# Sample attention of a hybrid decoder step: a fourth buffer for gathered cache rows, gathers issued behind the window loads, and the Silu of the output gate after the stage

## The chip, the core and the metric

The kernel runs on one NeuronCore of a Trainium2 chip. Five engines work side by side, each with its own instruction queue: TensorE (PE) multiplies and transposes into PSUM, VectorE (DVE) and ScalarE (ACT) do elementwise work, GpSimd (POOL) does elementwise work and issues the gathers, and SyncE (SP) issues the plain transfers. They meet at semaphores. The metric is the time of one launch in microseconds.

## What is computed

One step of a decoder trunk: a prompt of 512 tokens and eight samples of one new token each go through an input projection, sparse attention in three branches, a Mamba-2 scan (SSD), an output projection and an MLP. The change lies in the attention of the eight samples. Each sample reads its selected rows out of a paged cache, and its window rows out of a buffer:

```python
full_s = jnp.concatenate([paged_rows(cache_s), kv_s], axis=1)
idx = select_blocks(p_cmp, qpos, -(-(past + T) // SEL_BLOCK))
o_sel = selected_attention(q, idx, full_s, qpos)
win_rows = jnp.concatenate([win_buf.astype(x.dtype), kv_w], axis=1)
o_win = window_attention_rows(q, win_rows, qpos, kpos)
attn = gate_branches(gates, o_cmp, o_sel, o_win)
...
y = y.reshape(B, L, D_INNER) * jax.nn.silu(z.astype(f32))   # SSD output gate
```

PAST_LEN is 1024, WINDOW is 512, there are 16 heads over 4 key/value groups of 64 columns, all in float32. Of the past of a sample every block but one is selected, so a gather fetches all 1024 rows of the sample and a mask drops one block.

## The kernel before, in words

The program is written by hand, engine by engine: each engine's instructions run in the order in which its functions are written, and every crossing between engines is a semaphore wait. There is no scheduler.

The prompt's attention (`att_pe`, `att_act`, `att_dve`) ends at about 896 us of the span. The samples' stage (`smp_pe`, `smp_act`, `smp_dve`, `smp_sp`, `smp_pool`) follows it, and then the scan (`ssd_pe` and its kin), the output projection and the MLP.

For sample b the stage needs two tiles. The **gathered rows** (2 MB, 16 KB in each of 128 partitions) come by an indirect DMA that POOL issues (L1425). They have three places: `SEL = (sel_t[:, 0], sel_x, sel_t[:, 1])`, place b % 3. The **window rows** (1 MB) come by four plain DMAs that SP issues (L1408 and L1411) into `win_t`, which has three places too. Both kinds of transfer for sample b wait until `values(b - 3)` has been done on PE (`n_v`), since it is the last reader of the place.

PE runs a loop over the samples. In pass b it does: `fill(b + 1)`, that is six groups of four 128x128 transposes which turn the keys of the next sample (groups 0 to 3 from the gathered rows, 4 and 5 from the window rows, L1466); `turn_p(b)`, which transposes the probabilities (L1485); `scores(b + 1)` (L1476); `values(b)` (L1495). The six groups of `fill` use three PSUM banks in turn. Each is copied out before group x + 3 may start: the even groups by ACT (`key_copy`, L1574), the odd ones by DVE (L1628). ACT also takes the exponentials (L1579), copies the output of the sample before (`out_copy`, L1611) and the turned probabilities (L1597); DVE adds the mask and takes the maximum (L1681, L1686).

Work of the scan is laid into the passes. PE transposes pieces of the convolved input: `xs_turn` (L2163), eight `x_chunk_turn` (L2170), two `b_turn` (L2180) and `c_turn` (L2186). DVE scales the eight chunks (`x_scaled`, L2024), which also frees PSUM bank 7 for the next piece; ACT copies the two `b_turn` results (`b_copy`, L2114) and applies Silu to the eight tiles of the gate z, two in each of the passes 3 to 6 (L1587). After the loop DVE works out the factors of the three branches (`part_factors`, L1732 to L1765), PE computes `c_products` (L2193) and the samples' outputs (L1549, L1555), and the scan starts with `chunk(0)` (L2216). POOL prepares selector tiles for the scan (`ssd_pool`, L1877 to L1885) in memory that the gathered rows have left.

## Time and profile before

| | us |
|---|---|
| median of 3 runs | 2793.37 |
| lowest, highest | 2791.44, 2794.19 |
| the profiled execution, as timed | 2792.03 |
| its span in the profile | 2790.3 |
| PE busy | 2645.6 (95%) |
| DVE, ACT, POOL busy | 1128.8, 854.6, 107.3 |

The page of the profile cuts the span into 40 slices of 70 us. PE is busy for nine tenths or more in nearly all of them; the slices at 840 to 1120 us are those with 7 and 8 tenths, and the samples' stage from 896 to 1003 us is in these. The times below are positions in the span, read from the timelines of the engines. A row of a timeline gives start, duration, engine, line, operation, tiles and count; square brackets at its end hold how long the engine sat idle before it, and what ended that.

### The profile page before, as it was taken

How to read it: one execution, taken by the hardware profiler on the slowest of the kernel's cores; microseconds unless marked ns; L12 is line 12 of the kernel's file. 1: busy time of each engine (PE TensorE's matmuls, PEld its weight loads, DVE VectorE, ACT ScalarE, POOL GpSimd, SP SyncE). 2: the span in 40 equal slices, each digit the busy share in tenths (PEclk: the TensorE clock that was granted, in tenths of full speed). 3: DMA queues.
4: the chain of work that ended last, by engine and by line, in shares of the span. 5: the costliest groups of instructions: out<-in, count | busy, mean ns of one | idle time of the engine just before them, and what ended most of it. 6: DMA issues, size and time to landing. Idle time of an engine off the chain costs nothing.

```text
span 2790.3 us, 50995 instructions
## 1 busy us (share of the span) xinstructions
PE 2645.6 (95%) x21237; PEld 2531.0 (91%) x21237; DVE 1128.8 (40%) x1703; ACT 854.6 (31%) x1373; POOL 107.3 (4%) x116
## 2 busy tenths in 40 slices
PE   7889999998699788999999999999999999999998
PEld 6779999998577557998999999999999999999998
DVE  4432224554676577433333333333333233333333
ACT  3242112223575445322212212222122122221233
POOL 0000000000000041110000000000000000000011
PEclk9999999999799888999999999999999999999999
DMA  5154333233003743322322222222222222222222
GB/s 214 61 171 152 96 90 90 74 100 101 3 31 95 221 140 123 97 91 77 95 90 93 90 90 90 90 90 90 94 94 90 90 90 90 90 90 93 94 90 86
DMA packets 241815, 274.64 MB, mean 98 GB/s; under 512 B 19397, under 2 KB 233811, under 8 KB 237494
## 3 DMA queue, kind: packets, MB, share of 16 engines
q1 hardware_dynamic: 238966, 237.88, 27.3%
q0 software_dynamic: 1728, 33.56, 3.2%
q10 hardware_dynamic: 1040, 2.10, 0.3%
q8 instruction: 54, 0.88, 0.1%
q14 instruction: 27, 0.22, 0.0%
HBM read 261.10 MB, written 20.71 MB: 101 GB/s over the span
## 4 chain that ended last, share of the span: by engine, by line
PE 60%; DVE 2%; ACT 1%; issue 1%; DMA 0%; POOL 0%; ACTq 0%; POOLq 0%; DVEq 0%
PE PS L677 58%; DMA sel_x<-in_cache_kv_sel,idx_s 0%; PE PS L2735 0%; ACT sqr L2648 0%; ACT w_hi L658 0%; PE PS L2337 0%; DVE dec L2072 0%; DVE tmp_s L2307 0%; PE PS L2483 0%; DVE ys L2310 0%; ACT u_hi L2650 0%; DVE u_lo L2666 0%; DVE relu L2661 0%; PE PS L2216 0%; PE PS L2256 0%
## 5 line engine op out<-in xcount | busy, mean ns | idle before, releaser
L664 DVE TENSOR_TENSOR w_lo<-w_raw,w_hi 128x1024 fp32r<-128x1024 f32 (+1 forms) x388 | 460.3, 1190 | 1321.8 <-ACT w_hi L658 1320.8
L658 ACT ACTIVATE w_hi<-w_raw 128x1024 fp32r<-128x1024 f32 (+1 forms) x388 | 395.5, 1024 | 1481.1 <-PE PS L677 1480.8
L677 PE MATMUL PS<-h_hi,w_hi 128*128 128x260 f32 x3360 | 675.5, 283 | 8.0 <-DVE h_lo L591 3.6
L677 PE MATMUL PS<-h_lo,w_hi 128*128 128x260 f32 x3360 | 674.9, 282 | 0.0
L677 PE MATMUL PS<-h_hi,w_lo 128*128 128x260 f32 x3360 | 673.8, 282 | 0.0
L677 PEld LDWEIGHTS PS<-h_hi,w_hi 128*128 128x128 f32 x3360 | 516.3, 189 | 9.3 <-DVE h_lo L591 3.7
L677 PEld LDWEIGHTS PS<-h_lo,w_hi 128*128 128x128 f32 x3360 | 519.0, 189 | 0.0
L677 PEld LDWEIGHTS PS<-h_hi,w_lo 128*128 128x128 f32 x3360 | 517.8, 189 | 0.0
L677 PE MATMUL PS<-u_hi,w_hi 128*128 128x260 f32 x2048 | 411.1, 282 | 8.4 <-DVE u_lo L2666 8.4
L677 PE MATMUL PS<-u_lo,w_hi 128*128 128x260 f32 x2048 | 410.5, 282 | 0.0
L677 PE MATMUL PS<-u_hi,w_lo 128*128 128x260 f32 x2048 | 410.0, 281 | 0.0
L677 PEld LDWEIGHTS PS<-u_hi,w_hi 128*128 128x128 f32 x2048 | 313.7, 188 | 10.0 <-issue 10.0
L677 PEld LDWEIGHTS PS<-u_lo,w_hi 128*128 128x128 f32 x2048 | 315.3, 188 | 0.0
L677 PEld LDWEIGHTS PS<-u_hi,w_lo 128*128 128x128 f32 x2048 | 314.8, 188 | 0.0
L677 PE MATMUL PS<-mix_hi,w_hi 128*128 128x260 f32 x512 | 103.4, 284 | 7.5 <-DVE w_lo L664 7.5
L677 PE MATMUL PS<-mix_lo,w_hi 128*128 128x260 f32 x512 | 103.3, 283 | 0.0
L677 PE MATMUL PS<-mix_hi,w_lo 128*128 128x260 f32 x512 | 103.0, 283 | 0.0
L2556 DVE TENSOR_TENSOR x_acc<-PS,x_acc 128x520 f32 (+1 forms) x144 | 93.5, 691 | 11.2 <-PE PS L677 11.2
L677 PEld LDWEIGHTS PS<-mix_hi,w_hi 128*128 128x128 f32 x512 | 79.1, 190 | 7.6 <-issue 7.6
L1280 ACT ACTIVATE prob<-PS,negmax 128x128 f32<-128x128 f32 (+3 forms) x128 | 65.8, 525 | 49.3 <-DVE negmax L1310 49.3
L677 PEld LDWEIGHTS PS<-mix_lo,w_hi 128*128 128x128 f32 x512 | 79.5, 190 | 0.0
L677 PEld LDWEIGHTS PS<-mix_hi,w_lo 128*128 128x128 f32 x512 | 79.3, 190 | 0.0
(449 smaller groups left out, 2326.9 us busy)
## 6 DMA issues: line engine op xcount, KB each, us to landing
w_raw<-in_w_up SPq DMA_DIRECT2D x256, 256.0 KB, 2.8
w_raw<-in_w_down SPq DMA_DIRECT2D x256, 256.0 KB, 2.9
w_raw<-in_w_in SPq DMA_DIRECT2D x160, 256.0 KB, 2.9
w_raw<-in_w_out SPq DMA_DIRECT2D x64, 256.0 KB, 3.0
out_kv_win_s<-in_state_kv_win SPq DMA_DIRECT2D x8, 1022.0 KB, 7.5
win_t<-in_state_kv_win SPq DMA_DIRECT2D x8, 896.0 KB
xtok<-in_x_prompt SPq DMA_DIRECT2D x4, 1024.0 KB, 8.2
st_s<-in_state_ssm SPq DMA_DIRECT2D x8, 512.0 KB, 4.9
```

What stands on the lines that cost most here:

```text
L658: ins = e.activation(hi, raw, ACT.Copy)
L664: ins = e.tensor_tensor(lo, raw, hi.bitcast(F32), ALU.subtract)
L677: mm = e.matmul(PS[:, bank + 2 * m + h, 0:HN], w, x[:, k0 + k, h * HN:h * HN + HN], start=st and c == 0, stop=sp and c == 2)
L1280: e.activation(prob[:, u % 2, P_OFF[qt]:P_OFF[qt] + w], PS[:, qt, 0:w], ACT.Exp, bias=negmax[:, u % 2, qt:qt + 1], accum_out=den[:, u % 2, ...
L2556: e.tensor_tensor(x_acc[:, tile], PS[:, bank:bank + 2, 0:HN], x_acc[:, tile], ALU.add).then_inc(g_out, 1)
```

## The change

1. **A fourth place.** `sel_y` lies in memory that later holds `xdt`, the output of `x_scaled`. The places are now `SLOT = (0, 1, 2, 3, 0, 1, 2, 0)` for samples 0 to 7. The gather for sample 3 goes into `sel_y` and waits for the end of the prompt's attention (`as_o`), no longer for `values(0)`.
2. **Order of the gathers.** The gathers for samples 4, 5 and 6 wait for `values` 0, 1 and 2 (the samples that held places 0, 1 and 2), the one for sample 7 for `values(4)`. Each of these four also waits until the window load of the sample before it (3, 4, 5, 6) has landed. The waits of the window loads themselves are as they were.
3. **Silu after the stage.** The eight Silu instructions leave passes 3 to 6 and run on ACT after the last `out_copy`.
4. **The scan's pieces are laid out anew.** Since `xdt` may be written only after `values(3)`, the two `b_turn` come first (after `values(2)` and in pass 3), and the chunk turns run in passes 4 to 7, the last two of them in pass 7. DVE's `x_scaled` moves with them: chunks 6 and 7 are scaled inside `part_factors`. `ssd_pool` waits for `values(6)` in place of `values(5)`.

```diff
-        SEL = (sel_t[:, 0], sel_x[:], sel_t[:, 1])
+        sel_y = at("sel_y", [P, 8, KVW], A0 + 8 * TILE)
+        SEL = (sel_t[:, 0], sel_x[:], sel_t[:, 1], sel_y[:])
+        SLOT, USE = (0, 1, 2, 3, 0, 1, 2, 0), (1, 1, 1, 1, 2, 2, 2, 3)
...
             for b, dead in enumerate((2 * NU, 4 * NU - 8, 4 * NU)):
                 e.wait_ge(*as_s(dead))
-                gather(b, b)
-            for b in range(3, NB):
-                e.wait_ge(n_v, b - 2)
-                gather(b, b % 3)
+                gather(b, SLOT[b])
+            e.wait_ge(as_o, NH // 2)
+            gather(3, SLOT[3])
+            for b in range(4, NB):
+                e.wait_ge(n_v, SLOT.index(SLOT[b], 4 if b == 7 else 0) + 1)
+
+                e.wait_ge(nw_ld[(b - 1) % NS], 64 * ((b - 1) // NS + 1))
+                gather(b, SLOT[b])
...
-                elif 3 <= b < 7:
-                    x_chunk_turn(e, 2 * b - 5)
-                elif b == 7:
+                elif b == 3:
                     b_turn(e, 1)
-                    c_turn(e)
-                    e.transpose(PS[0:NB, 0, 0:96], stat[QR, 0, :], ident[QR, QR])
-                    e.transpose(PS[0:NB, 0, 96:192], stat[QR, 1, :], ident[QR, QR]).then_inc(n_stT.sem, 1)
+                elif b >= 4:
+                    if b == 7:
+                        e.transpose(PS[0:NB, 0, 0:96], stat[QR, 0, :], ident[QR, QR])
+                        e.transpose(PS[0:NB, 0, 96:192], stat[QR, 1, :], ident[QR, QR]).then_inc(n_stT.sem, 1)
+                    x_chunk_turn(e, 2 * b - 8)
+                    if b == 7:
+                        x_chunk_turn(e, 7)
+                        c_turn(e)
...
-                elif 2 <= b < 6:
-                    x_chunk_turn(e, 2 * b - 4)
-                elif b == 6:
+                elif b == 2:
                     b_turn(e, 0)
+                elif 4 <= b < 7:
+                    x_chunk_turn(e, 2 * b - 7)
...
-                elif 3 <= b < 7:
-                    for k in (2 * b - 6, 2 * b - 5):
-                        e.activation(pt[:, T_Z + k, :], pt[:, T_Z + k, :], ACT.Silu).then_inc(f_z.sem, 1)
-                elif b == 7:
+                elif b == 3:
                     b_copy(e, 0)
...
             out_copy(e, NB - 1)
+            for k in range(8):
+                e.activation(pt[:, T_Z + k, :], pt[:, T_Z + k, :], ACT.Silu).then_inc(f_z.sem, 1)
...
-                elif 3 <= b < 7:
-                    x_scaled(e, 2 * b - 6)
+                elif b >= 5:
+                    x_scaled(e, 2 * b - 9)
...
-                elif 3 <= b < 7:
-                    x_scaled(e, 2 * b - 5)
+                elif 4 <= b < 7:
+                    x_scaled(e, 2 * b - 8)
...
             ch.step(e.tensor_tensor(two(fac_T[:, 64:96]), two(den_s[:]), both(gate_b[:, :, 2]), ALU.mult))
+            x_scaled(e, 6)
+            x_scaled(e, 7)
             e.wait_ge(n_e, 1)
...
-            e.wait_ge(n_v, 6)
-            for x, count in enumerate((3, 3, 2)):
+            e.wait_ge(n_v, 7)
+            for x, count in enumerate((3, 2, 2, 1)):
```

POOL's queue, the gathers for samples 2 to 7, before (`n_v` counts `values`; the number behind a tile's name is its allocation):

```order
L1425 DMA sel_t_166<-in_cache_kv_sel,idx_s_55 128x4096 [waits pe_done_1]
L1425 DMA sel_t_166<-in_cache_kv_sel,idx_s_55 128x4096 [waits n_v]
L1425 DMA sel_x_167<-in_cache_kv_sel,idx_s_55 128x4096 [waits n_v]
L1425 DMA sel_t_166<-in_cache_kv_sel,idx_s_55 128x4096 [waits n_v] x2
L1425 DMA sel_x_167<-in_cache_kv_sel,idx_s_55 128x4096 [waits n_v]
```

The same place of POOL's queue now (`nw_ld0` to `nw_ld2` count the window loads landed in each of their three places):

```order
L1427 DMA sel_t_166<-in_cache_kv_sel,idx_s_55 128x4096 [waits pe_done_1]
L1427 DMA sel_y_168<-in_cache_kv_sel,idx_s_55 128x4096 [waits as_o]
L1427 DMA sel_t_166<-in_cache_kv_sel,idx_s_55 128x4096 [waits nw_ld0,n_v]
L1427 DMA sel_x_167<-in_cache_kv_sel,idx_s_55 128x4096 [waits nw_ld1,n_v]
L1427 DMA sel_t_166<-in_cache_kv_sel,idx_s_55 128x4096 [waits nw_ld2,n_v]
L1427 DMA sel_t_166<-in_cache_kv_sel,idx_s_55 128x4096 [waits nw_ld0,n_v]
```

The gather for sample 3 has moved from behind `values(0)` to the end of the prompt's attention, and the four behind it have a second wait each.

ACT's queue, pass 4 of the samples' loop, before (`pr` is the exponential, `o_t` the output copy, `proj` the gate z under Silu, `kT` the key copies, `prT` the turned probabilities):

```order
L1579 ACT_TABLE_LOAD
L1579 ACTIVATE pr_180,stat_177<-pr_180,stat_177 96x512 [waits n_max]
L1611 ACTIVATE o_t_168<-PS 96x256 [waits n_v]
L1587 ACT_TABLE_LOAD
L1587 ACTIVATE proj_64<-proj_64 128x520 x2
L1574 ACTIVATE kT_179<-PS 128x512 [waits n_fill,pe_done_1]
L1574 ACTIVATE kT_179<-PS 128x512 [waits n_fill] x2
L1597 ACTIVATE prT_181<-PS 128x384 [waits n_v,n_pT]
```

The same pass now:

```order
L1589 ACTIVATE pr_181,stat_178<-pr_181,stat_178 96x512 [waits n_max]
L1621 ACTIVATE o_t_169<-PS 96x256 [waits n_v]
L1584 ACTIVATE kT_180<-PS 128x512 [waits n_fill,pe_done_1]
L1584 ACTIVATE kT_180<-PS 128x512 [waits n_fill] x2
L1604 ACTIVATE prT_182<-PS 128x384 [waits n_v,n_pT]
```

Two table loads and two Silus have left the pass, and the key copies stand right behind the output copy.

DVE's queue from the last maximum to the wait for ACT's exponentials in `part_factors`, before (`st8` to `f_T_s` are the factors, `xdt` the scaled chunks):

```order
L2024 TENSOR_TENSOR xdt_208<-PS,dta_218 128x4x128 [waits d_pe_done]
L1681 TENSOR_TENSOR pr_180<-PS,dropq_174 96x512 [waits n_pT,pe_done_1]
L1686 TENSOR_REDUCE stat_177<-pr_180 96x1 [waits n_add]
L1732 COPY st8_191<-PS 8x192 [waits n_pe_end]
...
L1742 RECIPROCAL den_s_185<-st8_191 8x32
L1744 TENSOR_TENSOR f_T_s_189<-den_s_185,gate_b_178 8x32 [waits dve_ch]
L1746 TENSOR_TENSOR es_s_190<-e_s_187,st8_191 8x64 [waits n_e]
```

The same place now:

```order
L1691 TENSOR_TENSOR pr_181<-PS,dropq_175 96x512 [waits n_pT,pe_done_1]
L1696 TENSOR_REDUCE stat_178<-pr_181 96x1 [waits n_add]
L2036 TENSOR_TENSOR xdt_209<-PS,dta_219 128x4x128 [waits d_pe_done]
L1742 COPY st8_192<-PS 8x192 [waits n_pe_end]
...
L1752 RECIPROCAL den_s_186<-st8_192 8x32
L1754 TENSOR_TENSOR f_T_s_190<-den_s_186,gate_b_179 8x32 [waits dve_ch]
L2036 TENSOR_TENSOR xdt_209<-PS,dta_219 128x4x128 [waits d_pe_done] x2
L1758 TENSOR_TENSOR es_s_191<-e_s_188,st8_192 8x64 [waits n_e]
```

Three scalings now stand behind the last maximum, two of them between the factors.

## Rows read from the trace of the kernel before

**Rows 1.** Chain that ended last, in order of time: start us, us, what

```profile
968.42 13.68 DMA sel_x<-in_cache_kv_sel,idx_s
...
1097.04 152.96 PE PS L677 x1269
```

**Rows 2.** Timeline of PE through the samples' stage

```profile
943.96 0.66 PE L2170 MATMUL PS<-ident,proj 128*128 128x128 f32 x4
948.39 3.67 PE L1466 MATMUL PS<-ident,sel_x 128*128 128x128 f32 x16 [3.77 <-DMA sel_x<-in_cache_kv_sel,idx_s]
...
962.13 0.66 PE L1466 MATMUL PS<-ident,sel_t 128*128 128x128 f32 x4 [1.97 <-ACT kT L1574]
...
968.07 0.66 PE L2170 MATMUL PS<-ident,proj 128*128 128x128 f32 x4
970.88 3.58 PE L1466 MATMUL PS<-ident,sel_t 128*128 128x128 f32 x16 [2.15 <-DMA sel_t<-in_cache_kv_sel,idx_s]
...
979.79 0.66 PE L2170 MATMUL PS<-ident,proj 128*128 128x128 f32 x4
982.14 2.22 PE L1466 MATMUL PS<-ident,sel_x 128*128 128x128 f32 x16 [1.70 <-DMA sel_x<-in_cache_kv_sel,idx_s]
...
989.64 0.66 PE L2180 MATMUL PS<-ident,proj 128*128 128x128 f32 x4
```

**Rows 3.** Timeline of POOL, the gather of sample 3, the scan's first and fourth instruction

```profile
919.49 0.94 POOL L1425 DMA_INDIRECT sel_t<-in_cache_kv_sel,idx_s  x1 [33.01 <-PE PS L1495]
...
982.66 1.81 POOL L1877 MEMSET sel_h<- 128x2048 f32 x1 [13.31 <-issue]
...
989.57 1.17 POOL L1885 TENSOR_SCALAR_AFFINE_SELECT sel_p<-sel_p 16x1024 f32<-16x1024 f32 x1
```

**Rows 4.** Timeline of SP's queue, window loads of samples 0 and 5

```profile
896.18 1.11 SPq L1408 DMA_DIRECT2D win_t<-in_state_kv_win  x3
...
944.07 1.90 SPq L1408 DMA_DIRECT2D win_t<-in_state_kv_win  x3
```

**Rows 5.** Gathers of samples 2, 5 and 6: count, us from issue to landing

```profile
sel_t<-in_cache_kv_sel,idx_s POOLq DMA_INDIRECT x1, 8.6
...
sel_t<-in_cache_kv_sel,idx_s POOLq DMA_INDIRECT x1, 14.0
...
sel_t<-in_cache_kv_sel,idx_s POOLq DMA_INDIRECT x1, 12.3
```

**Rows 6.** DMA queues in 921:923, 944:946, 946:948: packets, MB, share of 16 engines

```profile
q1 hardware_dynamic: 81, 0.66, 103.9%
...
q0 software_dynamic: 41, 0.43, 52.3%
...
q0 software_dynamic: 2, 0.02, 2.8%
```

**Rows 7.** Timeline of ACT, pass 4 and the end of the stage

```profile
959.14 1.28 ACT L1587 ACT_TABLE_LOAD   x1
960.43 1.16 ACT L1587 ACTIVATE proj<-proj 128x520 f32<-128x520 f32 x2
...
1005.71 0.87 ACT L2128 ACTIVATE ebc<-PS 128x384 f32<-128x384 f32 x2 [9.58 <-PE PS L2202]
```

**Rows 8.** Timeline of DVE, a scaled chunk and the end of the factors

```profile
986.05 0.69 DVE L2024 TENSOR_TENSOR xdt<-PS,dta 128x512 f32<-128x512 f32 x1
...
995.13 0.28 DVE L1760 TENSOR_TENSOR pnz<-den_s,ident 8x128 f32<-8x128 f32 x1
```

**Rows 9.** PE's first reading of window rows, and its statistics transposes

```profile
904.42 1.95 PE L1466 MATMUL PS<-ident,win_t 128*128 128x128 f32 x8
...
991.60 0.25 PE L1534 MATMUL PS<-ident,stat 96*8 96x96 f32 x1
```

**Rows 10.** Windows: us, busy (x) by engine, PEclk, DMA share, GB/s

```profile
965.00:980.00 15.00, 12.79 (x110) 8.79 (x105) 6.36 (x10) 8.30 (x13) 0.94 (x1) 0.89 0.98 318
...
972.00:974.00 2.00, 2.00 (x11) 2.00 (x10) 0.69 (x1) 0.95 (x2) 0.00 (x0) 0.50 1.15 299
```

More of the change, by code:

```diff
@@ L1386, in build_program @@
         smn = at("smn", [P, 2], MF + 11360)
-        n_ld = [sem(f"n_ld{x}") for x in range(3)]
+        n_ld = [sem(f"n_ld{x}") for x in range(4)]
         nw_ld = [sem(f"nw_ld{x}") for x in range(NS)]
@@ L1992, in xs_scaled @@
             x = xdt_s[half]
-            e.wait_ge(*d_xT(half + 1))
+            e.wait_ge(*d_xsT(half + 1))
             ch.settle()
@@ L2022, in x_scaled @@
             c, half = f // 2, f % 2
-            e.wait_ge(*d_xT(f + 3))
-            e.tensor_tensor(xdt_c(c)[:, 4 * half:4 * half + 4], by_pair(PS[:, 7, :]),
+            e.wait_ge(*d_xT(f + 1))
+            e.tensor_tensor(xdt_c(c)[:, 4 * half:4 * half + 4], by_pair(PS[:, 4 if f == 7 else 7, :]),
                             per_head(dta[:, c, 0, 8 * half:8 * half + 8]).to_broadcast([P, 4, 2, HD]),
@@ L2163, in xs_turn @@
                 last = e.transpose(PS[0:NB, 7, x * P:x * P + P], xa[:, 4 * half + x, SEQ:NT], ident[:])
-            last.then_inc(d_xT.sem, 1)
+            last.then_inc(d_xsT.sem, 1)
         def x_chunk_turn(e, f):
             c, half = f // 2, f % 2
-            e.wait_ge(*d_xdt(f + 2))
+            if f == 0:
+                e.wait_ge(*d_btok(2))
+            elif f < 7:
+                e.wait_ge(*d_xdt(f + 2))
+            else:
+                e.wait_ge(n_ev_a, 3 * NB)
+                e.wait_ge(n_ev_d, 3 * NB)
             for x in range(4):
-                last = e.transpose(PS[:, 7, x * P:x * P + P], xa[:, 4 * half + x, c * P:c * P + P], ident[:])
+                last = e.transpose(PS[:, 4 if f == 7 else 7, x * P:x * P + P],
+                                   xa[:, 4 * half + x, c * P:c * P + P], ident[:])
             last.then_inc(d_xT.sem, 1)
@@ L2174, in b_turn @@
             e.wait_ge(*d_xa(12))
[L2175 removed]
             if f:
[L2177 to L2178 removed]
+                e.wait_ge(*d_btok(1))
+            else:
+                e.wait_ge(*d_xdt(2))
             for x in range(4):
[L2180 removed]
+                last = e.transpose(PS[:, 7, x * P:x * P + P],
                                    xa[:, 8 + x % 2, (2 * f + x // 2) * P:(2 * f + x // 2) * P + P], ident[:])
```

42 lines of the change are left out of this document (20 added, 22 removed).

## The prediction

> **What bounds the kernel now.** I read the chain of waits first, since it says which work sets the end. From 1097 us on it is all PE, and right before the scan it runs through one transfer: the gather for sample 7, issued at 968.42 and landed 13.68 us later [rows 1]. So the end of the samples' stage moves the end of the kernel one for one: behind it stand chains of PE, DVE and ACT with no slot in time of their own. The question is only when that stage ends.
>
> Next the timeline of PE through the stage. Write F(b) for the start of `fill(b)` and V(b) for the end of `values(b)`, which is where the next transposes start. The rows give V(2) = 943.96, F(4) = 948.39, V(4) = 968.07, F(6) = 970.88, V(5) = 979.79, F(7) = 982.14 and V(6) = 989.64 [rows 2]. Three fills begin late because a gather is late: 3.77 us at F(4), 2.15 at F(6), 1.70 at F(7), 7.6 us in all. A fourth wait is ACT's: in `fill(5)` the fourth group stands 1.97 us for a key copy [rows 2], and ACT was then busy with a table load of 1.28 us and two Silus of 1.16 us [rows 7].
>
> A pass costs, when nothing is late: F(7) to V(6) is 7.50 us, and a chunk turn of 0.66 behind it makes 8.2. After a long stop it costs more: F(6) to V(5) is 8.91 us [rows 2], and the granted clock there is 0.50, that is 1.2 GHz, though it is 1.00 elsewhere in the pass [rows 10].
>
> Last the transfers. A gather is 128x4096 floats (2.1 MB), a window load half of that, so a sample needs 3.15 MB. The stretch 965 to 980 shows the 16 engines 0.98 busy at 318 GB/s [rows 10]: 3.15 MB take 9.9 us, more than the 8.2 us of a free pass. Alone a gather lands after 8.6 us; beside a window load it takes 12.3 to 14.0 us [rows 5]. In 921 to 923, right after sample 3's gather was issued along with a window load, all the traffic is the window's (q1, 0.66 MB) [rows 6]. **So once the waits are gone the transfers are the next bound.** That decides the size of the gain.
>
> **The change part by part.**
>
> *Gather 3 early.* It now leaves at about 896.2, with the window loads of samples 0 to 2 [rows 4]. With its own 2.1 MB and three window loads the engines have 5.3 MB to move, 17 us at 318 GB/s, so it is down by 914, before V(0), and is read only two passes later. Gain by itself: nothing, since gather 3 was in time. What it buys is the idle time of the transfers that followed, for gathers 4 to 6.
>
> *Gathers 4 to 6.* Gather 4 needs V(0), about 919.2 (sample 3's gather left at 919.49 on it [rows 3]), and window load 3, issued then. No row shows a window load alone to its landing; bounds are 4 us (1.05 MB at 318 GB/s with the start left out) and 9 (the longest gather less the rate above). I take 6.5, since its data would be through in four to five. Gather 4 leaves at about 926 and lands by 936, where it is wanted at V(2) + 0.66 = 944.6. So F(4) moves from 948.39 to 944.6. `b_copy(0)` stands before the key copies in that pass, 0.55 us, and the turn of 1.16 us for two Silus is not there. V(3) = 944.6 + 7.5 + 0.55 = 952.7, say 953. Gather 5 leaves when window load 4 has landed, at about 941, and shares the engines with window load 5 from 945 on [rows 4]. By its own 8.6 us it lands at 949.6, by 12.3 at 953.3. F(5) = 953.0 to 953.5. No Silu stands before its key copies, so the 1.97 us go, and **V(4) = 953.3 + 7.5 = 961, against 968.07**.
>
> *Gather 6, the place where it is decided.* It leaves when window load 5 is down, at about 954, along with window load 6 (issued at V(3)). A pair takes 12.3 to 14 us: it lands at 966.3 to 968. F(6) would want it at 961.7. The window load of sample 7 goes out at V(4) = 961, into this gather's last third. What does an arriving window load do to a gather under way? The nearest row: in 944 to 946, with window load 5 just begun, the gather of sample 4 moved 0.43 MB, and in the 2 us after that only its last 0.02 MB [rows 6]. These last packets came late, but they were few. If the gather keeps its place, 966.3; if it stands still for the whole window load (1.05 MB, 3.3 to 4.2 us), 970.5. I take **F(6) = 967.5**, nearer the first, since the rows show two packets delayed and no large part of a gather. PE has then stood 5.9 us, and I charge the pass at its slow length of 8.91 us: V(5) = 976.4, and with the chunk turn F(7) can be 977.1.
>
> *Gather 7.* It waits for V(4) as before; window load 6 is down by then or 2 us later. It leaves at 961.2 to 963, five to seven us before 968.42 [rows 1]. But gather 6 and window load 7 are ahead of it: from 967 less the landing, 966, another 9.9 us and some 0.8 to land give 976.7. So **F(7) = 977.1 against 982.14: 5.0 us gained**, PE and transfers arriving together. V(6) = 984.6.
>
> *The end of the stage.* DVE has three scalings of 0.69 us [rows 8] behind the last maximum where it had none: the fifth waits for the chunk turn behind `values(6)`, the others stand between the factors. Two of them lie before the last factor, 1.38 us, which was done at 995.4 [rows 8]. Against this the statistics transposes stand ahead of the other turns and no longer at 991.60 [rows 9]: 0.75 us earlier. Net +0.65 us on the way to the factors. PE itself has one 0.6 us turn more before `values(7)`. Either way **0.7 us lost**; bounds 0 (both covered) and 1.4 (nothing of the order helps).
>
> *Silu.* Eight of them are 4 x 1.16 = 4.6 us, with a table load of 1.28 before and one after: 7.2 us of ACT. They stand in the 9.58 us in which ACT waited for the scan's first product [rows 7]. Covered with 2.4 us to spare, and the results are wanted 70 us later. If that cover went, up to 7.2 us would be on the path. The Trainium skill, page "ScalarE: Activation LUTs", section on what a table load costs, puts a switch at about 2.66 us, since a drain goes with the load of 1.28. The trace shows the load, and Silu starting 0.01 us after it. By the page the eight Silus and two switches are 9.9 us, and the scan would start some 0.4 us later; the sum would be that much worse.
>
> *POOL.* `ssd_pool` now waits for V(6) and not V(5). Its four instructions ran from 982.66 to 990.74 [rows 3], 8.1 us; from V(6) = 984.6 they end at 993, and the scan's first product, seen by ACT at 1005.71 [rows 7], comes at about 1001. Covered by 8 us. Behind the gathers with their new waits POOL has nothing else queued.
>
> **Sum:** 5.0 - 0.7 = 4.3 us. The profiled execution took 2792.03 (span 2790.3), which would become 2787.7 (2786.0). The median is 2793.37, 1.3 above it; 2793.37 - 4.3 = **2789.1 us**. About 0.2%, 5.6 us, is what a measurement can tell from no change, so this is inside it.
>
> **The rivals.**
>
> *A. The transfers pair up well.* Gather 6 lands at 965.5, the clock stays up (pass 8.2), and gather 7 takes from V(4) what it takes now: 961 + 0.2 + 13.68 = 974.9. Then F(7) = 975, gain 7.2 - 0.7 = 6.5: 2786.9, and 2786 at best. For it: 13.68 us already includes a window load beside it and a rest of gather 6. Against it: gather 6 would have to be through by 965, and 9.9 us for each pair leave no room.
>
> *B. Engines share packet by packet.* The Trainium skill, "DMA: Bandwidth & Descriptors", section on queues, rings and completion order, says that each DMA engine goes round the queues that have work, a packet at a time. The trace does not agree in the first 2 us of a pair, where the gather gets nothing [rows 6], but may for one under way. As a mechanism here: gather packets are 16 KB (0.43 MB with small ones among 41) against 8 KB of the window loads (0.66 MB in 81), so a gather would take two thirds. Gather 6 keeps moving and lands at 967. But window load 0, read at 904.42 [rows 9], now has gather 3 beside it from 898: at a third of the rate its remaining 0.9 MB take 9 us and not 3; it lands at 907 to 908, and everything behind it shifts by up to 3.6 us. The passes shift; gather 7, wanted at about 980, comes with them. Gain 5.0 - 0.7 - 2.5 to 3.6 = 0.7 to 1.8: 2792.
>
> *C. Slower: window loads starve gather 6.* If each window load takes the engines for its whole life of 9 us (small pieces included), gather 6 stands from 962 to 970 and lands at 973. F(6) is 973.2 against 970.88 now, V(5) 982.1, F(7) 982.8, the end 0.6 + 0.7 = 1.3 us later: 2794.7; with B's shift added, 2797. It decides from F(6) = 971.6 on: 971.6 + 8.91 + 0.66 - 982.14 + 0.7 = -0.3, about even. For it: the first 2 us of a pair. Against it: the gather of sample 6 moved on while the next window load began, and landed after 12.3 us.
>
> *D. Nothing moves.* If landing of the window loads is slow (9 us or more), gathers 4 and 5 leave at 928 and 943, gather 5 is 2 us late and gather 6 leaves at 957: F(6) = 970, F(7) = 980. Gain 2 - 0.7 = 1.3: 2792.
>
> **How the numbers follow.** The forecast (F(6) between 966 and 969, gain 3 to 5.6) 0.48; A 0.22; B and D together 0.22; C 0.08. The forecast's own range is 2787.8 to 2790.4. Eight in ten takes in A to its best end and D, B, and C's near part: 2786.0 to 2794.6. Faster by over 5.6 us is most of A: 0.23. Slower by over 5.6 us needs C and B together: 0.04. The rest, 0.73, is within 0.2%.
>
> **What would show it.** In the profile after: the first DMA stall of PE at F(6), of 3 to 8 us, and none at F(4); V(4) at 960 to 962; at F(7) a stall under 2 us; key copies in `fill(5)` without the 2 us wait; ACT's idle time before the scan's first exponential down from 9.58 to 1 to 3 us; the last factor of DVE 6.4 us after V(6). The transfers should be busy without a gap from 955 to 976. I am wrong in size if F(6) is before 965 or after 971, and in mechanism if PE's first window transposes (904.42) come later, if the scan waits for ACT or POOL, or if gather 5 is late by more than 1 us.

## The result and the profile after

The changed kernel takes 2796.99 us (median of 20 runs, 2790.87 to 2799.87) against 2793.34 for the kernel before, run beside it on the same chip (20 runs, 2787.70 to 2797.26). The ratio is 1.0012, with an interval of 1.0006 to 1.0017: some 3.5 us slower, less than the 0.2% within which the forecast counts a time as the same, but on the other side of zero, and outside both of the forecast's ranges (2787.8 to 2790.4, and the wide one, 2786.0 to 2794.6). The profiled execution took 2799.59 us, with a span of 2797.9, which is 2.6 us above its own median; the one of before was 1.3 below its median. So the two traces are 7.6 us apart where the medians are 3.7 apart, and I use the traces to place the loss, and the medians for its size.

The first view is again the chain of waits (start us, us, what). It still goes through the gather of sample 7. In the kernel before it then stays on PE until the scan; now it runs through DVE behind the stage, and for longest through two steps on `den_s`:

```profile
967.80 12.03 DMA sel_t<-in_cache_kv_sel,idx_s
...
994.75 2.01 DVE den_s L1760
996.78 1.20 DVE den_s L1762
...
1104.21 184.99 PE PS L677 x1536
```

`den_s` is a tile of 8 x 32 numbers. The weights phase starts at 1104.21, against 1097.04 in [rows 1].

The timeline of PE at the places of [rows 2] and [rows 9]:

```profile
906.75 1.97 PE L1473 MATMUL PS<-ident,win_t 128*128 128x128 f32 x8 [1.17 <-DMA win_t<-kvs_tok]
...
958.43 3.48 PE L1473 MATMUL PS<-ident,sel_x 128*128 128x128 f32 x16 [7.16 <-DMA sel_x<-in_cache_kv_sel,idx_s]
...
979.87 3.68 PE L1473 MATMUL PS<-ident,sel_t 128*128 128x128 f32 x16 [4.16 <-DMA sel_t<-in_cache_kv_sel,idx_s]
...
989.69 0.66 PE L2188 MATMUL PS<-ident,proj 128*128 128x128 f32 x4
...
999.29 0.24 PE L1557 MATMUL PS<-ident,f_T_s 8*96 8x8 f32 x1 [2.79 <-DVE pnz L1772]
...
1000.52 7.01 PE L1565 MATMUL PS<-sel_f,o_t 96*128 96x16 f32 x32
```

The stops at F(4) and F(6) are gone, as forecast. Two longer ones, 7.16 us at F(5) and 4.16 at F(7), stand where 7.6 us stood in three. V(6) is 989.69. This execution entered the stage 0.89 us later than the other (first fill at 896.93 and not 896.04), so in its own time the stage gained 0.8 us. And then PE stands 2.79 us for DVE, where it did not stand in the kernel before.

DVE at that place (the rows that answer to [rows 8]), then POOL (to [rows 3]):

```profile
991.74 0.18 DVE L1747 TENSOR_TENSOR neg_m<-neg_m,neg_new 8x32 f32<-8x32 f32 x1
...
992.69 1.27 DVE L2036 TENSOR_TENSOR xdt<-PS,dta 128x512 f32<-128x512 f32 x2
993.88 0.83 DVE L1758 TENSOR_TENSOR es_s<-e_s,st 8x64 f32<-8x64 f32 x1
994.75 2.00 DVE L1760 TENSOR_TENSOR den_s<-es_s 8x32 f32<-8x32 f32 x1
996.78 1.19 DVE L1762 TENSOR_TENSOR den_s<-den_s,e_s 8x32 f32<-8x32 f32 x1
...
998.96 0.28 DVE L1772 TENSOR_TENSOR pnz<-den_s,ident 8x128 f32<-8x128 f32 x1
```

```profile
989.85 1.81 POOL L1889 MEMSET sel_h<- 128x2048 f32 x1 [21.11 <-PE PS L1502]
991.59 0.95 POOL L1890 MEMSET sel_p<- 128x1024 f32 x1
992.62 4.10 POOL L1894 TENSOR_SCALAR_AFFINE_SELECT sel_h<-sel_h 16x2048 fp32r<-16x2048 f32 x2
996.78 1.17 POOL L1897 TENSOR_SCALAR_AFFINE_SELECT sel_p<-sel_p 16x1024 f32<-16x1024 f32 x1
```

`es_s` is a product of 8 x 64 numbers, the two `den_s` are sums of 8 x 32. In the kernel before they took 0.20, 0.18 and 0.18 us:

```profile
993.75 0.18 DVE L1748 TENSOR_TENSOR den_s<-es_s 8x32 f32<-8x32 f32 x1
```

Now they take 0.83, 2.00 and 1.19, and they end at 994.71, 996.75 and 997.97. POOL's three selects end at 994.67, 996.72 and 997.95 (the first two are one row, x2, and are taken as halves of it). Each of the three ends with a select. `neg_m`, beside POOL's second memset, kept its 0.18 us, and the two scalings at 992.69, which read PSUM beside the first select, kept their pace too (1.27 us for both, 0.69 for one). The last factor is ready 9.55 us after V(6); in [rows 8] with [rows 2] it was 5.77.

What that does to the clock is in the windows (us, busy of each engine, then granted clock, DMA share, GB/s), first of the kernel before, then of the changed one:

```profile
1000.00:1005.00 5.00, 5.00 (x12) 2.65 (x12) 3.95 (x13) 0.00 (x0) 3.08 (x1) 0.50 0.06 12
1005.00:1010.00 5.00, 5.00 (x24) 3.01 (x23) 0.94 (x2) 0.87 (x2) 3.48 (x3) 0.98 1.08 281
1010.00:1015.00 5.00, 3.39 (x6) 0.93 (x5) 4.93 (x7) 2.29 (x8) 0.00 (x0) 0.70 1.20 321
```

```profile
1000.00:1005.00 5.00, 5.00 (x24) 4.78 (x24) 4.86 (x10) 2.46 (x4) 2.00 (x1) 0.50 0.00 0
1005.00:1010.00 5.00, 5.00 (x15) 3.52 (x16) 2.19 (x12) 0.00 (x0) 1.65 (x1) 0.50 0.00 0
1010.00:1015.00 5.00, 5.00 (x8) 1.67 (x6) 0.84 (x2) 0.98 (x2) 2.54 (x3) 0.50 0.98 256
```

After the stop the granted clock is 0.50, that is 1.2 GHz, for all three windows; before it was 0.50 in the first alone, 0.98 and 0.70 in the others. The engine has work to do in all of them: the 32 products of the outputs took 5.3 us before and take 7.0. ACT (to [rows 7]) has its first exponential of the scan at 1011.89, 6.2 us later:

```profile
995.57 1.28 ACT L1617 ACT_TABLE_LOAD   x1
996.86 4.32 ACT L1617 ACTIVATE proj<-proj 128x520 f32<-128x520 f32 x8
...
1011.89 0.98 ACT L2140 ACTIVATE ebc<-PS 128x384 f32<-128x384 f32 x2 [9.40 <-PE PS L2222]
```

So between the two traces: 0.89 us are the stage's later start, -0.84 the stage, 3.78 the factors, 2.35 what follows them up to the first exponential (12.65 us against 10.30), 1.0 the scan, and 0.4 the rest: 7.6. Only the terms of 3.78 and 2.35 are larger than what executions of the same code differ by, as the table of the next section shows.

### The profile page after: what moved, and what is told of

Read it like the earlier page. It is cut to its first block, busy times and chain, and to the rows that moved or that the text cites. A ratio compares the mean times of both kernels' runs of the same rounds, so it can differ in the third digit from the quotient of the medians.

```text
span 2797.9 us, 50994 instructions
## 1 busy us (share of the span) xinstructions
PE 2648.7 (95%) x21237; PEld 2534.8 (91%) x21237; DVE 1131.3 (40%) x1703; ACT 847.1 (30%) x1367; POOL 107.2 (4%) x116
## 4 chain that ended last, share of the span: by engine, by line
PE 60%; DVE 2%; ACT 1%; issue 1%; DMA 0%; POOL 0%; ACTq 0%; POOLq 0%; DVEq 0%
PE PS L677 57%; DMA sel_t<-in_cache_kv_sel,idx_s 0%; PE PS L2755 0%; ACT sqr L2668 0%; ACT w_hi L658 0%; PE PS L2236 0%; PE PS L2357 0%; PE PS L1565 0%; DVE dec L2084 0%; DVE tmp_s L2327 0%; PE PS L2503 0%; DVE ys L2330 0%; ACT u_hi L2670 0%; DVE u_lo L2686 0%; DVE relu L2681 0%
```

## The experiments

Each was timed in 5 rounds beside the kernel before, and the ratio is to that kernel in the same rounds, with a 95% interval. The rounds were run at different times and on different chips, so two variants are compared by their ratios. E of a trace is its first exponential of the scan less its first fill, which takes the start of the stage out. In us:

| | first fill to V(6) | V(6) to the last factor | from there to the first exponential | E |
|---|---|---|---|---|
| before | 93.60 | 5.77 | 10.30 | 109.67 |
| e2, before with POOL late | 93.45 | 10.09 | 12.56 | 116.10 |
| changed | 92.76 | 9.55 | 12.65 | 114.96 |
| e9, PE kept busy | 89.50 | 9.54 | 9.87 | 108.91 |
| e8, POOL behind the factors | 93.26 | 6.08 | 13.91 | 113.25 |
| e10, fills beside the factors | 94.15 | 6.08 | 12.51 | 112.74 |
| e1, POOL early | 89.43 | 6.10 | 10.65 | 106.18 |

The changed kernel, e8, e9 and e10 run the same instructions up to V(6), and yet their stages take 89.5 to 94.2 us. **So the stage of a single trace can't be told from another's within 4 to 5 us.** By V(2) they are already 3.2 us apart (44.1 to 47.3 us after the first fill): two of the slower three had a granted clock of 0.77 to 0.89 over 935 to 945, the third 0.66 at 915 to 920 and at 935 to 940, where e9 had 1.00. What follows the first exponential took 1784.5 to 1791.4 us in the 13 traces. The middle columns repeat well: the way to the last factor is 9.0 to 9.6 us in the four traces of the changed kind where POOL's selects fall on it (changed, e3, e9, e12) and 6.1 in the five where they don't (e1, e5, e6, e8, e10). The conclusions on POOL below rest on these columns, those on the stage on much less.

**e1, POOL early.** Samples 5 and 6 exchange places, so that the memory of `sel_h` is free after V(5), and POOL waits for that:

```diff
-        SLOT, USE = (0, 1, 2, 3, 0, 1, 2, 0), (1, 1, 1, 1, 2, 2, 2, 3)
+        SLOT, USE = (0, 1, 2, 3, 0, 2, 1, 0), (1, 1, 1, 1, 2, 2, 2, 3)
@@ ssd_pool
-            e.wait_ge(n_v, 7)
+            e.wait_ge(n_v, 6)
```

> Edit: the changed kernel with places 1 and 2 exchanged for samples 5 and 6, so that POOL's selector work for the scan waits for values(5) and not values(6). Theory 1 (POOL's fills and selects run at the same time as DVE's factors on 8 partitions and stretch them: three adds took 0.83, 2.00 and 1.19 us instead of 0.20, 0.18 and 0.18): POOL starts with the landing of the last gather, about 980, and is done by 988; the three are back at 0.2 us, the last factor ends 6.3 to 6.6 us after values(6) and not 9.5, PE no longer stands 2.8 us there, and the time is 4 to 7 us below the changed kernel, 2790 to 2793. Theory 2 (the loss is the late gather 5 and lower clock of its own accord): nothing changes in the time behind values(6), 2796 to 2797.

Measured: 2789.13 against 2792.75, ratio 0.9989 (0.9980 to 0.9998). POOL's work is over before the factors begin, the additions are back at 0.18 us, and V(6) is 985.25, 89.43 us after the first fill (93.60 before). PE stood 5.39 us at F(5) and 3.69 at F(7). POOL, then ACT:

```profile
978.28 4.08 POOL L1894 TENSOR_SCALAR_AFFINE_SELECT sel_h<-sel_h 16x2048 fp32r<-16x2048 f32 x2
```

```profile
1002.00 0.87 ACT L2140 ACTIVATE ebc<-PS 128x384 f32<-128x384 f32 x2 [3.96 <-PE PS L2222]
```

With one engine's 8 us put elsewhere, the change makes the kernel faster by 3.6 us in the medians (0.6 to 5.6 by the interval) instead of slower by 3.7. Not all of that difference can be put on POOL. Behind V(6) this trace is 5.45 us shorter than that of the changed kernel, 3.45 to the last factor and 2.0 after it; that part is POOL's. Its stage is 3.3 us shorter as well, but 2.4 of these it is ahead at V(2), before the exchange of places can act, and e9 had as short a stage with POOL late. ACT still waits 3.96 us for PE after its Silus: they are covered.

**e2, the other way round.** The kernel before, with only POOL's wait changed:

```diff
@@ ssd_pool
-            e.wait_ge(n_v, 6)
+            e.wait_ge(n_v, 7)
```

> Edit: the kernel before, with one number changed: POOL's selector work waits for values(6) and not values(5). Theory 1: POOL starts at 989.9 instead of 982.7, meets DVE's factors, stretches them by 3 to 4.5 us; with the lower clock that follows, 4 to 7 us slower than before. Theory 2: POOL is covered by 8 us, no change (within 1 us).

Measured: 2799.60, ratio 1.0028 (1.0016 to 1.0039). One number in a wait costs 6.9 us in the medians, 7.8 by the ratio (4.5 to 10.9). E is 6.4 us longer, all of it behind V(6). Of the experiments this is the cleanest: nothing else is changed. The selects now meet other operations, and each of these again lasts until a select ends (993.66, 995.70). DVE, then POOL:

```profile
991.62 2.04 DVE L1737 TENSOR_TENSOR neg_m<-neg_m,neg_new 8x32 f32<-8x32 f32 x1
993.70 2.07 DVE L1739 TENSOR_TENSOR e_s<-neg_m,st 8x64 f32<-8x64 f32 x1
```

```profile
991.62 4.08 POOL L1882 TENSOR_SCALAR_AFFINE_SELECT sel_h<-sel_h 16x2048 fp32r<-16x2048 f32 x2
```

The factors are ready 10.1 us after V(6), and the scan's first exponential comes 22.65 us after it (16.07 before).

**e8, POOL behind the factors.** The changed kernel; POOL also waits for `pnz`:

```diff
@@ ssd_pool
+            e.wait_ge(*n_fac(1))
             ch.step(e.memset(sel_h[:].bitcast(F32), 1.0))
```

> The changed kernel with one line more: POOL's four selector instructions also wait for the last factor of DVE (pnz). Everything else, places, order, waits of the gathers, stays. Theory 'POOL beside DVE's small operations': the sums es_s and den_s are back at 0.20, 0.18 and 0.18 us, pnz ends 6.0 to 6.5 us after V(6) and not 9.5, PE doesn't stand 2.8 us for it, its clock stays up, and POOL's 8.1 us end at about V(6) + 14.3, a microsecond before the scan's first product wants them: 3 to 7 us back of the 2797.0, that is 2790 to 2794. Rival 'it is the new order of DVE and PE at the end (two scalings and two turns more), POOL only happens to run': pnz stays at 9 us or more after V(6), 2797. Rival 'the collision only moves': POOL then runs beside the masking and the scaling of the first chunk (0.63 and 1.2 us each), these stretch and the scan's first products come as late as now, 2796.

Measured: 2796.05, ratio 1.0011 (1.0002 to 1.0020). The factors are back at 6.1 us behind V(6), which rules out that DVE's or PE's new order made them late. But the time hardly moves, because the rival that the collision only moves was right. DVE, POOL, and what PE then waits for:

```profile
999.76 1.98 DVE L2027 SCALAR_TENSOR_TENSOR ones<-ones,top_end,ones 128x128 fp32r<-128x128 f32 x1
1001.78 2.43 DVE L2031 TENSOR_TENSOR bct<-bct 8x512 fp32r<-8x512 f32 x1
```

```profile
999.51 4.16 POOL L1895 TENSOR_SCALAR_AFFINE_SELECT sel_h<-sel_h 16x2048 fp32r<-16x2048 f32 x2
```

```profile
1006.46 3.59 PE L2237 MATMUL PS<-xdte,b_tok 128*128 128x512 f32 x4 [2.91 <-DVE xdte L2054]
```

The two took 0.35 and 0.68 us in the changed kernel. The first product of the scan waits for what stands behind them. The select of `sel_p` (1003.73, 1.51 us) then met the scaling `xdte` (3.21 us for two, 2.36 in the changed kernel). At each of the places behind V(6) that were tried (here, in e2, e10 and the changed kernel) the selects met DVE work that the scan waits for.

**e10, fills beside the factors.** The changed kernel; POOL fills as now, fills `sel_h` twice more, and selects only after `pnz`:

```diff
@@ ssd_pool
             ch.step(e.memset(sel_p[:], 1.0))
+            for _ in range(2):
+                ch.settle()
+                ch.step(e.memset(sel_h[:].bitcast(F32), 1.0))
             ch.settle()
+            e.wait_ge(*n_fac(1))
```

> The changed kernel; POOL fills its selectors as now, right after V(6), then fills sel_h two more times (1.8 us each, of no use), so that it is busy for 6.4 us beside all the factors; its three affine_selects wait for the last factor. In the trace of the changed kernel es_s, den_s and den_s took 0.83, 2.00 and 1.19 us and ended at 994.71, 996.75 and 997.97, which is where POOL's three affine_selects ended (994.67, 996.72, 997.95); small operations of the same kind beside POOL's memset had kept their 0.18 us, and so had the scalings that read PSUM. Theory 'a DVE operation with two inputs in SBUF waits out a POOL instruction that reads SBUF': with fills alone beside them es_s and den_s take 0.20, 0.18 and 0.18 us, pnz ends 6.1 to 6.5 us after V(6); the selects then collide with the next SBUF operations of DVE (ones_2, bct) as in the run with POOL behind the factors, but end 2.8 us earlier, V(6) + 12: chunk 0 waits less than 2.9 us, the scan's first exponential stands 17.5 to 19 us after V(6) (20.0 there), 2793 to 2795. Rival 'any work of POOL slows DVE's SBUF operations': es_s, den_s stretched by the fills, pnz 9 us or more after V(6), 2797 or more. The Trainium skill, page 'SBUF — State Buffer', section 'Who interferes with whom', states the first: two SBUF inputs of DVE contend with a GpSimd instruction that reads SBUF, not with one that only writes it.

Measured: 2795.85, ratio 1.0010 (1.0001 to 1.0019), a microsecond above the top of what was expected, the mechanism as expected. DVE, then POOL:

```profile
994.26 0.18 DVE L1760 TENSOR_TENSOR den_s<-es_s 8x32 f32<-8x32 f32 x1
...
998.79 1.85 DVE L2028 TENSOR_SCALAR ones<-ones,top_end 128x128 fp32r<-128x128 f32 x1
```

```profile
992.74 3.67 POOL L1893 MEMSET sel_h<- 128x2048 f32 x2
996.48 4.07 POOL L1898 TENSOR_SCALAR_AFFINE_SELECT sel_h<-sel_h 16x2048 fp32r<-16x2048 f32 x2
```

A busy POOL did DVE nothing as long as it only wrote: 0.18 us in the midst of a fill of 1.8. The first DVE operation on SBUF under a select ends with it (1000.64; the selects of `sel_h` end at 1000.55). The Trainium skill, "SBUF — State Buffer", section "Who interferes with whom", has this rule: a DVE instruction with two SBUF inputs contends with a GpSimd instruction that reads SBUF, not with one that only writes, and the one that comes second stands until the other is through. The traces agree in every row of an instruction with two inputs in SBUF: 0.18 us beside fills, 2.0 under a select of 2.05. The row of `ones` above is not covered by the rule as it is told here: it has one tensor in SBUF and a column of factors, and was held up too (1.85 us, 0.29 in the changed kernel).

That the second stands for the first shows the other way round as well, in the kernel before. DVE's two scalings `xdte`, with two inputs in SBUF, start just ahead of POOL's scaling `bc_row`, which then takes 3.70 us; at 1008.21, with DVE idle, it takes 1.56:

```profile
999.31 2.36 DVE L2041 TENSOR_TENSOR xdte<-xdt,te 128x1024 f32<-128x1024 f32 x2
```

```profile
999.38 3.70 POOL L1897 TENSOR_SCALAR bc_row<-bct,of_smp 72x512 fp32r<-72x512 f32 x1 [8.64 <-DVE bct L2018]
...
1008.21 1.56 POOL L1897 TENSOR_SCALAR bc_row<-bct,of_smp 72x512 fp32r<-72x512 f32 x1
```

**e9, PE kept busy.** The changed kernel, with 18 transposes that nobody reads, in front of the wait for the factors:

```diff
             c_products(e)
+            for x in range(18):
+                e.transpose(PS[:, 1, 0:P], ident[:], ident[:])
             e.wait_ge(*n_fac(1))
```

> The changed kernel with 18 more transposes of PE into a bank that is free, put where PE stands 2.8 us for the last factor; about 2.6 us of work that nobody reads. POOL stays where the change puts it, so the factors stay 9.5 us behind V(6). Theory 'half of the loss is the factors' lateness, the other half the clock that falls after PE's stop': the 32 products of the outputs take 5.3 us and not 7.0, the chunk products 2.0 and not 3.8, the granted clock over 1000 to 1010 is near 1.00, and 3 to 4 us come back: 2793 to 2794. Rival 'the clock falls there for other reasons, as it did at 1000 to 1005 in the kernel before too': the low stretch stays, 2797. Rival: the granted clock's low stretch only moves behind the products, 2795 to 2796.

```profile
993.35 2.13 PE L1557 MATMUL PS<-ident 128*128 128x128 f32 x18
996.31 0.21 PE L1559 MATMUL PS<-ident,f_T_s 8*96 8x8 f32 x1 [0.83 <-DVE pnz L1774]
...
996.99 4.76 PE L1567 MATMUL PS<-sel_f,o_t 96*128 96x16 f32 x32
```

The factors are as late as in the changed kernel (9.5 us after V(6)), and the products behind them take 4.76 us, not 7.01; from the factors' end to the first exponential it is 9.9 us, not 12.65. So in the traces the clock is worth 2.8 us and goes with the stop. In the time little of it can be seen: 2795.92, ratio 1.0007 (0.9997 to 1.0016), 1.1 us below the changed kernel where 3 to 4 were expected, with intervals that overlap. That part of the gain stays unproven.

**e12, half the window rows.** The changed kernel; from sample 3 on a window load leaves out half of its large piece:

```diff
                 for p0, p1, nr in win_parts():
+                    if b >= NS and p0 == 0:
+                        p1 = 56
```

> The changed kernel with half the window rows: from sample 3 on the large piece of a window load takes 56 of its 112 partitions (what stays in the buffer is read in place of the rest, so the results of samples 3 to 7 are others); 0.46 MB less per sample, as many transfers. Theory 'transfers are the bound of the stage, a window load beside or ahead of a gather is what makes it late': a sample has 2.7 MB, 8.4 us at 318 GB/s against a pass of 8.2; window load 3 alone lands in 5 to 6 us and not 8.0, gather 5 leaves some 4 to 5 us earlier, the stops at F(5) and F(7) fall from 11.3 us to 3 to 6 in all, V(6) stands 86 to 89 us after the first fill (92.8 now), and with the collision of POOL and DVE still there 2791 to 2794. Rival 'landing is latency, not volume': window loads land as late as now, the stops stay at 10 us or more, 2796 to 2797.

```profile
953.12 2.06 PE L1475 MATMUL PS<-ident,sel_x 128*128 128x128 f32 x16 [1.54 <-DMA sel_x<-in_cache_kv_sel,idx_s]
...
963.88 3.62 PE L1475 MATMUL PS<-ident,sel_t 128*128 128x128 f32 x16 [2.66 <-DMA sel_t<-in_cache_kv_sel,idx_s]
```

The stops are 4.2 us in all and not 11.3, and V(6) is 84.9 us after the first fill: better than expected, and outside the 89.5 to 94.2 of the same code with all rows. So it is the bytes, and not the number of transfers, that make the rows late. The time is 2790.65 (ratio 0.9992, 0.9982 to 1.0003), with POOL and DVE still colliding. The DMA engines aren't full from end to end, though: in the trace of the changed kernel their share is 0.45 and 0.38 in the two windows from 920 to 930, where window load 3 moves alone while gather 4 waits for it, and 0.37 from 965 to 970.

**e3 and e5, without the order.** The changed kernel (e3), and e1 (e5), without the gathers' wait for a window load:

```diff
@@ smp_pool
-                e.wait_ge(nw_ld[(b - 1) % NS], 64 * ((b - 1) // NS + 1))
```

> Edit: the changed kernel without the wait of gathers 4 to 7 for the window load before them. Theory G (the added wait is what makes gather 5 late: window load 4 shares the engines with gather 4 and takes 12 us to land, and gather 5 leaves only then): gather 4 leaves at 922, gather 5 at 932 instead of 944, lands by 946, the 7.2 us stop of PE before fill(5) goes, values(6) ends 3 to 6 us earlier. Rival (the transfers are the bound anyway): fill(7) starts within 1 us of where it does with the wait, and the time is the same within 1 us, since later gathers stand longer by what the earlier ones gained.

> The changed kernel with POOL's selectors early (they wait for V(5), the places of gathers 5 and 6 exchanged) and, on top of that, without the wait of gathers 4 to 7 for the window load ahead. The run with POOL early and that wait kept stood at 2789.1 us, with stops of PE of 5.4 us at F(5) and 3.7 us at F(7). Theory 'the transfers are the bound, the order only deals the lateness out': the same sum of stops, now on window rows and gathers both, V(6) 89.0 to 90.3 us after the first fill, 2788.5 to 2790. Rival 'the order is what holds gathers 5 and 7 back': the gathers leave at V(0), V(1), V(2) and V(5), 5 to 10 us earlier, the stops shrink to 3 us in all, V(6) 84 us after the first fill, 2784. Rival 'the order protects the window rows, as it is meant to': window rows late by 5 us as in the run without the order before, 2792.

Measured: e3 2794.11 (ratio 1.0004, 0.9995 to 1.0012), e5 2791.87 (0.9989, 0.9978 to 1.0000; its neighbour e1 has 0.9989 too). The order keeps the window rows in time and gains nothing that can be measured. Without it gather 4 leaves at V(0) and gather 5 is in time, but it is the window rows of sample 5 that PE then waits for, in e3:

```profile
957.60 1.97 PE L1472 MATMUL PS<-ident,win_t 128*128 128x128 f32 x8 [4.72 <-DMA win_t<-kvs_tok]
```

The stops of e3's two late tiles come to 9.55 us, and those of the changed kernel to 11.3. In e5 no window rows are late: it stands 4.80, 1.51 and 3.24 us for gathers 5, 6 and 7, 9.6 in all, and e1 5.39 and 3.69, 9.1 in all. From first fill to V(6) e5 takes 89.3 us and e1 89.4. So leaving the order out moves the lateness to other tiles and doesn't remove it.

**e6, gather 3 later.** e1, with gather 3 behind window load 1:

```diff
@@ smp_pool
             e.wait_ge(as_o, NH // 2)
+            e.wait_ge(nw_ld[1], 64)
             gather(3, SLOT[3])
```

> POOL's selectors early, and the gather of sample 3 waits for window load 1 and no longer leaves with window load 0. It is the same place and the same buffer, some 8 to 15 us later, and is read 35 us later. Rival B's mechanism (the gather takes packets from window load 0, PE's first window transposes stood 1.2 us for it, and everything behind shifts) says: that wait goes, the stage starts 1.2 us earlier and so does its end: 2787.9, if nothing late in the stage takes it back. Theory 'transfers are the bound from gather 5 on': the wait goes, but gather 3 now pushes window loads 2 and 3 back, gather 4 leaves no earlier, and the 1.2 us come back as a longer stop at F(5): 2789 to 2790, no change against 2789.1.

Measured: 2793.12, ratio 1.0003 (0.9993 to 1.0013). Both theories missed: the wait of 1.2 us at the first window transposes did go, and the kernel was some 4 us slower than e1, with intervals that just overlap. V(6) is 93.7 us after the first fill; the granted clock was 0.51 from 925 to 935, where e1 has 1.00. In the eight traces with a stop of 0.9 to 1.5 us at 905, which all have gather 3 early, the granted clock was 1.00 from 921 to 936, though in four of them it fell for a shorter time before or after that stretch. In the four without it (the kernel before, e2, e4, e6) the mean over 921 to 936 was 0.66, that is 0.50 for some 10 of the 15 us; the text of e11 says 7, which is too few.

**e11, a stop put in.** To tell whether that stop spares the clock: the kernel before, where PE's first window transposes also wait for window load 1:

```diff
@@ fill
                         e.wait_ge(nw_ld[s], 64 * (b // NS + 1))
+                        if b == 0:
+                            e.wait_ge(nw_ld[1], 64)
```

> The kernel before with one wait more: PE's first window transposes (sample 0) also wait for window load 1, a stop of 1 to 2 us at about 905. Nothing is moved. In five traces with such a stop (0.9 to 1.5 us, all with gather 3 early) the granted clock was 1.00 from 915 to 935; in four without it (the kernel before, both variants of it, and the one with gather 3 held back) it fell to 0.50 for some 7 us between 920 and 935. Theory 'the stop at 905 is what spares the low stretch': V(2) comes no later than now in spite of the stop, and the low stretch at 922 to 933 is gone; what the later gathers do with it decides the rest, 2790 to 2793. Rival 'the low stretch belongs to something else, such as what gather 3 did to the turns': it stays, V(2) is 1 to 2 us later, 2794 to 2795.

```profile
910.29 1.94 PE L1468 MATMUL PS<-ident,win_t 128*128 128x128 f32 x8 [3.98 <-issue]
```

Measured: 2797.67, ratio 1.0015 (1.0006 to 1.0024). The stop came out at 4 us and not at 1 to 2, so this doesn't settle it. What speaks for the early stop: V(2) comes 48.3 us after the first fill, and 47.9 without the stop, so that of 4 us only 0.4 were left, and the granted clock over 925 to 935 was 0.81 to 0.85, though it had been at 0.50 to 0.52 from 905 to 915. What was won there was given back later, with 3.4 us at F(7). Whether the early stop or the early gather spares the clock stays open.

**e4, Silu alone.** The kernel before, with the eight Silus behind the last `out_copy`:

```diff
-                elif 3 <= b < 7:
-                    for k in (2 * b - 6, 2 * b - 5):
-                        e.activation(pt[:, T_Z + k, :], pt[:, T_Z + k, :], ACT.Silu).then_inc(f_z.sem, 1)
@@ behind the passes
             out_copy(e, NB - 1)
+            for k in range(8):
+                e.activation(pt[:, T_Z + k, :], pt[:, T_Z + k, :], ACT.Silu).then_inc(f_z.sem, 1)
```

(One more line, not shown, changes the order in which ACT's signals are counted to match.)

> Edit: the kernel before with only the eight Silus moved behind the stage. Expected by my prediction: the 1.97 us wait in fill(5) goes, but gathers 6 and 7 stay the bound: V(4) 2 us earlier, gather 7 leaves 2 us earlier; the scan's first exponential does not wait for ACT. 1 to 2 us faster than before. Rival: ACT is late for the scan (table loads cost more than the 1.28 us they show): 0.5 us or more slower, with ACT's idle time before the first exponential gone.

Measured: 2793.05, ratio 0.9998 (0.9989 to 1.0007): the same, where 1 to 2 us faster was expected. The 1.97 us in `fill(5)` went, and the gather of sample 6 took them: PE stood 4.64 us for it, 2.15 in [rows 2]. ACT still had 2.54 us to spare before the scan.

## Why the prediction was wrong

**The step that failed is POOL.** The text took its 8.1 us from the row, added them to V(6), compared the end with the time at which the scan wants the product, and said "covered by 8 us". That deadline was right: PE never waited for a selector, and so the text's own sign, the scan waiting for POOL, would not have caught it. But a cover has two sides. I asked who waits for POOL, and not who works beside it and on what memory. In the kernel before the selects ran from 985.43 to 990.74 [rows 3], and in that stretch DVE had nothing that reads two inputs from SBUF: a key copy, a scaling and a mask, which read PSUM, and a reduction with one input:

```profile
985.28 0.69 DVE L1628 COPY kT<-PS 128x512 f32<-128x512 f32 x1 [0.18 <-PE PS L1466]
...
988.03 0.69 DVE L1681 TENSOR_TENSOR pr<-PS,dropq 96x512 f32<-96x512 f32 x1 [1.29 <-PE PS L1476]
988.75 0.68 DVE L1686 TENSOR_REDUCE stat<-pr 96x1 f32<-96x512 f32 x1
```

A few more rows of the trace would have told me that the work was moved from a place where DVE works from PSUM to one where it works from SBUF. In the traces the two terms behind V(6) grew by 3.8 us at the factors and 2.35 after them, and e1, which has the change without the collision, keeps 0.33 and 0.35 of these. So the collision cost 3.45 and 2.0 us, the second by the lower clock, as e9 shows; e2, with nothing else changed, puts it at 6.9 us in the medians. The rule was to be had in the Trainium skill ("SBUF — State Buffer", "Who interferes with whom"), and it spoke against this change. I had no rival for it, nor for any loss behind V(6) beyond 1.4 us but Silu's, so the chances for slower, 0.08 for C and 0.04 for more than 5.6 us, had no mechanism of the right kind in them.

**Without that the sum comes out, but by luck where the stage is concerned.** e1 is the change with POOL's work off the factors: 2789.13 us measured, 2789.1 forecast. The tail costs 0.68 us there (16.75 us from V(6) to the first exponential, against 16.07), which is the 0.7 of the text. The stage is 4.2 us shorter than before in this trace, where the text had 5.0, but by another route, and the same code took from 89.5 to 94.2 us in others: against the 93.60 of before that is anything from a gain of 4.1 to a loss of 0.6. What the change gains in the stage isn't measured to better than that, and by its interval e1 as a whole is 0.6 to 5.6 us faster.

**Gathers 5 to 7: the right bound, at the wrong place.** The text had the first stop at F(6), and gather 5 late by 0. It was late by 7.16 us, and more than 1 us was named there as a sign of a wrong mechanism. The terms that were mis-sized are the window loads and the gather behind them: 6.5 us for a load alone. Window load 3 left at 921.82, and the gather that waits for it at 929.81; the next, beside gather 4, left at 932.02 and freed gather 5 at 944.38, 12.4 us later and not 941 as in the text. Gather 5 then took 14.0 us to land, where the text had 8.6 to 12.3. SP, then POOL (the rows that answer to [rows 4] and [rows 3]):

```profile
921.82 1.08 SPq L1410 DMA_DIRECT2D win_t<-in_state_kv_win  x3
...
932.02 1.18 SPq L1410 DMA_DIRECT2D win_t<-in_state_kv_win  x3
```

```profile
929.81 0.94 POOL L1427 DMA_INDIRECT sel_t<-in_cache_kv_sel,idx_s  x1 [31.55 <-DMA win_t<-kvs_tok]
944.38 0.94 POOL L1427 DMA_INDIRECT sel_x<-in_cache_kv_sel,idx_s  x1 [13.63 <-DMA win_t<-kvs_tok]
```

Rival D had 9 us or more for the window loads, and with them gathers at 928 and 943; it came nearest, in these two and in F(7) (980, measured 979.87), though it had gather 5 only 2 us late and gather 6 leaving at 957, and that left at 952.45. It made the stage gain 2 us, and in this trace it gained 0.8. I charged one slow pass, 8.91 us behind F(6), and there were two, 8.8 us behind F(5) and 9.8 behind F(7). The transfers were to be busy without a gap from 955 to 976; their share was 0.37 from 965 to 970.

**F(6), by accident.** Forecast 967.5, measured 967.68, but without a stop: V(4) was 967.19 and not 961, so late that gather 6 was in time.

**Rival B** had window load 0 up to 3.6 us late for the packets of gather 3. It was 1.2 us late, and window load 1 after it 0.8. The first window transposes came at 906.75, 1.4 us later after the first fill than before, which the text had named as a sign of a wrong mechanism. Of the cost that B gives it, nothing can be seen: without that wait (e6) the kernel was not faster.

**Silu** was right. The table load and the first Silu stand 0.01 us apart as before, the whole takes 6.9 us (995.57 to 1002.48; 7.2 in the text), and ACT waited for PE afterwards: 2.54 us in e4, 3.96 in e1. By the price of a switch in the Trainium skill ("ScalarE: Activation LUTs", what a table load costs) it would have been 9.9 us, an estimate; the traces don't show the part beyond the load.

**Two sums of the text don't close.** "Faster by over 5.6 us is most of A" has 0.23, more than the 0.22 of A itself. And the upper bound of 9 us for a window load doesn't come out of its working, the longest gather less the rate: at 318 GB/s, 14.0 less the 6.6 us of the gather's own bytes is 7.4, and less the 3.3 of a window load's 10.7. Neither moves the forecast.

## What to carry to other kernels

Before moving work of POOL, list what DVE does in the stretch it moves to, and from which memory. In these traces a POOL select held up each DVE operation with two inputs in SBUF until it ended, however small that one was, and a POOL scaling was itself held up by DVE's. Fills held up none of the DVE work beside them, and selects none that had an input in PSUM. A wait's number can hide such a placement, and "the result is wanted 8 us later" covers only one side of it. Where bytes bound a stage, as e12 showed for this one, ordering its transfers mostly picks the tile that is late. And before reading a gain of a few us off two traces, look at what the same instructions took in others: here up to 4.7 us more or less.

## What the runs showed of the hardware

- An addition of 8 x 32 numbers took 2.00 us of DVE under a POOL select of 2.05 us, and 0.18 beside a POOL fill of 1.8. In e10 a DVE operation with one tensor input in SBUF and a column of factors (`ones`, 128 x 128) was held up as well: 1.85 us against 0.29.
- The hold-up goes both ways: POOL's `bc_row` took 3.70 us when two DVE scalings with two SBUF inputs had started 0.07 us ahead of it, and 1.56 with DVE idle.
- After PE's stop of 2.8 us the granted clock was 0.50 for 15 us in which PE was always busy; with 2.1 us of transposes that nobody reads in front and a stop of 0.83 it was 0.95 over 995 to 1000, 0.50 over the next 5 us and 0.87 over the five after (e9).
- A window load (1.05 MB) with nothing beside it took 8.0 us from issue until its waiter went on; a gather with twice the bytes landed after 8.6 [rows 5]. With 0.46 MB less (e12) the window load's step took 6.3 us.
- Removing 1.2 us of waiting at 905 (e6) went with a granted clock of 0.51 at 925 to 935 and with 4 us lost against e1. Whether it is the stop that spares the clock stays open.
- The same instructions, in four traces, took 89.5 to 94.2 us from the first fill to V(6).
